# Four quads in place of three in the first pair of output chunks of two down projections

## What is computed

```python
def swiglu(x, w_gate, w_up, w_down):
    return (jax.nn.silu(x @ w_gate) * (x @ w_up)) @ w_down

h = layer_norm(DEEPNORM_ALPHA * h + 0.5 * swiglu(h, ffn1_w_gate[l], ffn1_w_up[l], ffn1_w_down[l]),
               ln1_g[l], ln1_b[l])
```

## Time and profile before

| | us |
|---|---|
| median of three runs | 1897.63 |
| the profiled execution | 1897.59 |
| its span | 1895.9 |
| TensorE matmul (PE) busy | 1878.3 (99%) |
| VectorE (DVE) busy | 1450.9 (77%) |
| ScalarE (ACT) busy | 970.4 (51%) |
| data moved | 357.51 MB, mean 189 GB/s |

### The profile page before, as it was taken

How to read it: one execution, slowest core, us unless ns; L and a number is a source line. 1 busy time by engine, 2 the same in 40 slices (tenths; PEclk the granted TensorE clock), 3 DMA queues, 4 the chain that set the end, 5 groups by cost and what they waited for, 6 DMA issues and landing times.

```text
span 1895.9 us, 28391 instructions
## 1 busy us (share of the span) xinstructions
PE 1878.3 (99%) x10382; PEld 1602.0 (84%) x10382; DVE 1450.9 (77%) x1637; ACT 970.4 (51%) x1094; POOL 66.9 (4%) x93
## 2 busy tenths in 40 slices
PE   9999999999999999999999999999999999999997
PEld 8888888888888888999999888888888888888886
DVE  5777777777788896677766967677777777688887
ACT  5555555554454554545744534445555555455452
POOL 0000000000000001300131100000000000000000
PEclk9999999999999999999999999999999999999999
DMA  8554555656655684755432067535665555646654
GB/s 309 168 178 177 186 208 212 216 206 223 201 177 189 209 310 120 220 180 151 131 133 91 23 211 256 177 123 207 214 215 193 188 181 195 223 136 219 217 182 189
DMA packets 185376, 357.51 MB, mean 189 GB/s; under 512 B 11328, under 2 KB 23616, under 8 KB 184272
## 3 DMA queue, kind: packets, MB, share of 16 engines
q1 hardware_dynamic: 183600, 347.43, 53.6%
q0 software_dynamic: 1696, 8.99, 1.4%
HBM read 354.28 MB, written 2.10 MB: 188 GB/s over the span
## 4 chain that ended last, share of the span: by engine, by line
PE 94%; DVE 4%; issue 1%; DMA 1%; ACT 1%; POOL 0%; POOLq 0%; DVEq 0%; ACTq 0%
PE acc L629 21%; PE acc L631 21%; PE acc L630 21%; PE acc L653 3%; PE acc L657 3%; PE acc L655 3%; PE acc L1268 2%; PE acc L1266 2%; PE acc L1267 2%; PE tp L1312 1%; PE tp L1310 1%; PE tp L1311 1%; PE tp L1193 1%; PE tp L1268 1%; PE tp L1267 1%; PE tp L1266 1%
## 5 line engine op out<-in xcount | busy, mean ns | idle before, releaser
L629 PE MATMUL acc<-whi,xT 128*128 128x512 f32 (+2 forms) x1132 | 429.5, 379 | 0.8 <-ACT zab L2107 0.4
L631 PE MATMUL acc<-whi,xT 128*128 128x512 f32 (+2 forms) x1132 | 426.2, 377 | 0.0
L630 PE MATMUL acc<-wlo,xT 128*128 128x512 f32 (+2 forms) x1132 | 425.9, 376 | 0.0
L1150 DVE TENSOR_TENSOR wlo<-raw,whi 128x1024 fp32r<-128x1024 f32 x248 | 303.2, 1222 | 146.0 <-ACT whi L1143 143.4
L617 DVE TENSOR_TENSOR wlo<-raw,whi 128x1024 fp32r<-128x1024 f32 (+2 forms) x239 | 277.9, 1170 | 154.3 <-ACT whi L601 152.9
L1143 ACT ACTIVATE whi<-raw 128x1024 fp32r<-128x1024 f32 x248 | 262.5, 1059 | 222.9 <-PE acc L631 139.3
L601 ACT ACTIVATE whi<-raw 128x1024 fp32r<-128x1024 f32 (+2 forms) x239 | 238.1, 1005 | 227.6 <-PE acc L631 159.8
L629 PEld LDWEIGHTS acc<-whi,xT 128*128 128x128 f32 x1132 | 212.6, 188 | 42.2 <-issue 1.7
L631 PEld LDWEIGHTS acc<-whi,xT 128*128 128x128 f32 x1132 | 212.6, 188 | 38.5
L630 PEld LDWEIGHTS acc<-wlo,xT 128*128 128x128 f32 x1132 | 212.7, 188 | 38.0
L629 PE MATMUL acc<-whi,hT 128*128 128x512 f32 x352 | 137.4, 390 | 1.0 <-DVE wlo L617 1.0
(11 more groups left out here) (433 smaller groups left out, 3387.5 us busy)
## 6 DMA issues: line engine op xcount, KB each, us to landing
raw<-in_ffn_w_down_dram SPq DMA_DIRECT2D x176, 512.0 KB, 6.8
raw<-in_ffn_w_up_dram SPq DMA_DIRECT2D x175, 512.0 KB, 8.4
raw<-in_ffn_w_gate_dram SPq DMA_DIRECT2D x174, 512.0 KB, 4.4
raw<-in_w_in_dram SPq DMA_DIRECT2D x48, 512.0 KB, 4.0
raw<-in_w_out_dram SPq DMA_DIRECT2D x32, 512.0 KB, 6.0
raw<-in_w_in_dram SPq DMA_DIRECT2D x32, 260.0 KB, 2.9
raw<-in_w_in_dram SPq DMA_DIRECT2D x16, 456.0 KB, 7.2
raw<-in_w_q_idx_dram SPq DMA_DIRECT2D x8, 512.0 KB, 3.5
```

The costliest lines, as they stand in the source:

```text
L629: pe.matmul(o, hi, w_hi[:, s, k, 0:width], start=first and k == 0, stop=False, skip_group_check=seeded)
L630: pe.matmul(o, hi, w_lo[:, s, k, 0:width], start=False, stop=False, skip_group_check=seeded)
L631: ins = pe.matmul(o, lo, w_hi[:, s, k, 0:width], start=False, stop=last and k == UNIT_KT - 1, skip_group_check=seeded)
L1150: dve.tensor_tensor(lo[:, s], src, hi[:, s].bitcast(F32), ALU.subtract).then_inc(lo_done, 1)
```

## The change

The first pair gets the same four quads as the second and the same plain units; its groups have two plain units each, so that a group reads unit, P1, P3, P5, unit, P7, P6, P2, P4. With 13 units at the head the pair has 56 items, and its tail starts at item 49 with seven items. As the tail is one item shorter, the folds take three items in place of four, in both pairs: 0, then 1, then 2 and 3 together, with the statistics behind them.

```diff
@@ -290,7 +290,7 @@
     QUADS = [(4 + q, 8 + q) for q in range(4)]
     QUAD_KT = 8
     ENDS = [*range(4), *range(12, DOWN_U)]
-    PAIRS = [Pair(QUADS[:3], sorted(ENDS + [7, 11]), sorted(ENDS + [7, 11]), 13, (4, 4, 4)),
+    PAIRS = [Pair(QUADS, ENDS, ENDS, 13, (2, 2, 2, 2)),
              Pair(QUADS, ENDS, ENDS, 2, (4, 4, 4, 4))]
     FOURTH_FROM = 16
     SPLITS, LAST_USER = split_slots(PAIRS, FOURTH_FROM, EDGES)
@@ -1777,9 +1777,11 @@
                     down_add(pair, 0, 0)
                 if i == 3:
                     down_add(pair, 0, 1)
-                if 4 <= i < 8:
+                if 4 <= i < 6:
                     fold(pair, i - 4)
-                if i == 7:
+                if i == 6:
+                    fold(pair, 2)
+                    fold(pair, 3)
                     for t in range(T):
                         down_stats(pair, 0, t)
```

## The result

The kernel with four quads takes 1901.17 us in the median of 20 runs (1900.55 to 1902.57), against 1897.78 us before (20 runs, 1896.98 to 1898.37). The ratio is 1.0018, with a 95% interval of 1.0012 to 1.0024: 3.4 us slower, and just inside the 0.2% that was taken for the same. The forecast was 1901.0 us. It removed twelve matmuls and TensorE was busy for longer: the page has 1880.8 us for it against 1878.3, with 12 fewer. (Its records overlap, so a short stall passes as busy time there.)

The account below looks back on a forecast made before the run. TensorE was taken to bound most stages, VectorE the quads, barely in time. Network 1 +1.8, network 2 +0.75 and landings +0.9 made +3.4 us on 1897.59: 1901.0 us, range 1896.5 to 1905.0.

Parts of the forecast that it names:

- (a): First pair: block (7, 11) becomes a quad, 42 matmuls for 48; saves 1.36 us per network, 2.72 us in all.
- (b): VectorE gets seven more operations per network; a group then needs 15.03 us of VectorE against 14.96 of TensorE.
- (c): The load of block (5, 1), issued behind P2's low half, makes the next P5 sum start at 15.92, not 15.03 us.
- (d): Network 1's first pair: +1.8 us, with the saved 1.36 us inside it and stalls of 3.2 us.
- (e): Network 2's first pair: +0.75 us, since the 1.03 us lost before to a late load is not lost twice.
- (f): Loads behind P2 in six turns: a mean landing of 4.36 us in place of 4.2 adds +0.9 us.
- (g): ScalarE's high halves in the quads: cost nothing, about 1 us of room at the tightest; 6 us if uncovered.
- (h): Folds in three steps at the pair's end: cost nothing, cover 3.2 us; 1.4 us per network if uncovered.
- Loads in time: Rival: the first load of a burst lands within 3.3 us; -2.8 us, 1894.8 us; chance 0.12.
- Late landings: Rival: first loads behind P2's low half take 5.5 us, not 4.2; with three 1904.1 us; three or more, chance 0.13.
- Folds uncovered: Rival: a burst delays the second pair by 1.4 us per network; +2.8 us more, 1903.8 us; chance 0.04.

Follow-up runs that it names:

- experiment 1: The changed kernel with the first pair's quad loads reordered, so that block (a, 1) no longer takes the slot that P2 frees: 1895.25 us, ratio 0.9988.
- experiment 2: The changed kernel with block (a, 1) loaded one place later, behind the unit, in the first pair: 1910.81 us, ratio 1.0071.
- experiment 5: The kernel before, still three quads, but in groups of two plain units in place of four: 1901.6 us, ratio 1.0018.
- experiment 4: The kernel before with the folds in three steps alone, still three quads in groups of four units: 1897.64 us, ratio 1.0001.
- e1: Same run as experiment 1: the changed kernel with the first pair's quad loads reordered; 1895.25 us, ratio 0.9988.
- e4: Same run as experiment 2: the changed kernel with block (a, 1) loaded one place later; 1910.81 us, ratio 1.0071.
- e5: Same run as experiment 3: the changed kernel with the sums for P7, P6 and P4 cut to 8 of each 512 columns; 1893.13 us, ratio 0.9978.
- e6: Same run as experiment 6: the changed kernel with reordered quad loads and the head's input sums one item earlier; 1893.26 us, ratio 0.9975.
- e7: The changed kernel, its loads in the order of the change, with the head's input sums one item earlier: 1898.59 us, ratio 1.0004.
- e2: Same run as experiment 4: the kernel before with the folds in three steps alone; 1897.64 us, ratio 1.0001.
- e3: Same run as experiment 5: the kernel before, three quads, in groups of two plain units; 1901.6 us, ratio 1.0018.
- e8: Same run as experiment 8: the kernel before with the head's input sums one item earlier; 1895.92 us, ratio 0.999.
- experiment 6: The changed kernel with the first pair's quad loads reordered and the head's input sums one item earlier: 1893.26 us, ratio 0.9975.
- experiment 3: The changed kernel with the sums for P7, P6 and P4 made on 8 of each 512 columns, waits and loads kept: 1893.13 us, ratio 0.9978.
- experiment 8: The kernel before with the sums of the inputs in the head one item earlier: 1895.92 us, ratio 0.999.

## Why the prediction was right

*(a), the saving.* TensorE without waits takes 115.15 us for the stretch against 117.23 before: 1.36 us for the six matmuls and 0.7 for the late start. The change by itself could reach only the former. (In network 2 the two late loads before, some 0.9 us, come on top.)

*(b) and (c), VectorE's turn and the load behind P2.* Offsets within quad 0's turn were right to 0.02 us: counted from the P5 sum, the changed kernel's P4 sum is at 9.26, P2's low half at 10.39, P1's at 13.88 us. The whole turn is 15.00 us in experiment 1 where 15.03 was written, and 15.85, 16.08 and 15.89 us in the changed kernel where 15.92 was. TensorE's stalls in network 1 were eight small ones, one at each quad's unit ahead of P7 and one at each P2, where six or seven were expected; they make 3.5 us where 3 us was written. Experiment 1 removes the load and the waits go, experiment 2 delays it and they grow, experiment 5 brings them with no quad added. This is shown, not argued.

*(d), network 1.* +1.8 us was written; the stretch grew from 117.23 to 119.03 us, +1.80.

*(e), network 2.* +0.75 us was written, +0.96 measured, the second turn's load having taken 4.5 us. The weak point is the kernel before, not the one after. Its 1.03 us were not one late load in quad 2 but two, 0.46 us in quad 1 and 0.47 us in quad 2. This step took them for the kernel's habit, and experiment 4 shows an execution with 0.4 us of it.

*(f), late landings.* +0.9 us was written for a landing of 5.5 us among the six. The profile after has none: they took 4.1, 4.4 and 4.2 us, and 4.2, 4.5 and 4.2 us, a mean of 4.27 us: by the term's own sum 6 x 0.07 = 0.4 us, and by the stretches 0.2 us, as (d) and (e) together measured 2.76 us where 2.55 was written. What made up the total is a cost that the prediction didn't have. The two stretches account for 1.80 + 0.96 = 2.8 us of the 3.7 us between the spans; 0.9 us lies elsewhere. The same sum for the others (difference of span less difference of stretches) gives +0.8 us in e1, +1.1 in e4, +1.2 in e5, +0.9 in e6, +1.4 in e7, but -0.3 in e2, +0.2 in e3 and -0.1 in e8. So every kernel with four quads in the first pair loses 0.8 to 1.4 us outside it, and none with three does. Some 0.3 us of it comes ahead of the down projection (its first matmul is at 482.4 to 482.7 us, against 482.1 to 482.2), most between the second pair of network 1 and network 2. TensorE's matmuls there are the same 6684, in the same order; only within the first 420, those of the second pair, do some use another split slot. Counted from the second pair's start, none of the delay arises in these. It comes later, in the mixer, in small stalls at the same matmuls of these kernels: in the profile after 0.3 us at 747.53, 0.2 us at 803.81, 0.3 us at 990.64 (this one varies from kernel to kernel, and experiment 6 has none) and 0.15 us at 1060.11. At the first, TensorE's weight load waits for a low half of VectorE; the second row is the same weight load before:

```profile
747.53 0.19 PEld L629 LDWEIGHTS acc<-whi,xT 128*128 128x128 f32 x1 [0.41 <-DVE wlo L617]
...
744.98 0.19 PEld L629 LDWEIGHTS acc<-whi,xT 128*128 128x128 f32 x1
```

Why that low half comes later stays open; no run was made for it. The total was right, then, with one term too large by 0.7 us and one of 0.9 us missing, and that they cancel is luck. The part that the mechanism explains is the 2.8 us of the stretches.

*(g), ScalarE, and (h), the folds.* No item of the quads waited on ScalarE for a slot. ScalarE isn't nothing, though: experiment 1 shows three starts of a turn late by 0.08 us each behind a high half just made, 0.24 us in all, which the rows that (b) copies from had in them already. The cover at the end of the pair was 3.3 us where 3.2 was written.

*Rivals.* Loads in time was the state of experiment 1, and its price, -2.8 us, came out at -2.35 (the stretches give -3.0 us; the rest is the loss outside them). Late landings didn't come by themselves; experiment 2 made them, with a load 1.3 us later on paper and 1.55 us lost per turn ((7.02 - 1.80 + 5.08 - 0.96) / 6, from the stretches). Folds uncovered fell: the second pair starts without a wait in the changed kernel and in experiments 1, 3 and 6.

*What the Trainium skill says.* The prediction quotes half of what "VectorE: DVE Perf Modes", section "The DRAIN you can't avoid", says. It has the next operation wait for an empty pipeline, and goes on in the same paragraph that an operation that is not held starts earlier. So its 15.9 us for a group isn't what the page gives, and the page isn't refuted. The turn of 15.00 us for thirteen operations in experiment 1, 1.15 us each with records of 1.22 us, agrees with the second half.

## What to carry to other kernels

Cheaper arithmetic on the bound engine moved work here to the engine that prepares its operands: six matmuls less on TensorE, seven operations more on VectorE. Before packing such blocks closer, add up both engines' time per block from start to start, not from record lengths: here 14.96 against 15.03 us left nothing over. In a ring of load slots, ask of each load whose slot it takes; a load that is needed first mustn't take the slot that is given back last. The saving was there all along, 0.25% instead of a loss of 0.18%, behind the order of one list and sums that stood one item too late. Of the 4.75 us of experiment 6, though, 1.9 us is to be had without a fourth quad, by experiment 8.

## What the runs showed of the hardware

In these traces a stall of TensorE costs more than the idle time shown. The profile's bracket says 0.31 us at 526.16, but the start is 0.47 us late against the pitch, the first matmul's record is 0.50 us long instead of 0.39, and the next start is 0.11 us late again. At P2 it shows no wait, and the start is 0.15 to 0.18 us late. Over network 1's first pair the view of waits gives TensorE 1.3 us, the starts give 3.5. The granted clock stayed at full speed through all of it (0.997 to 0.999 in every run).
